# A decoder layer on Trainium2: the output stage joined to the RWKV and end program

## The reference

```python
h = rmsnorm(x, g_pre)
s5_x, s5_z, rw_p, rw_z, pl_x, pl_z, gate_cols = split(h @ w_in)
u_s5 = (s5_mix(s5_x) * silu(s5_z)) @ w_up_s5
u_rw = (rwkv_mix(rw_p) * silu(rw_z)) @ w_up_rwkv
u_pl = (pool_mix(pl_x) * silu(pl_z)) @ w_up_pool
merged = gates[0] * u_s5 + gates[1] * u_rw + gates[2] * u_pl      # gates = sigmoid(gate_cols)
out = merged @ w_o
return x + rmsnorm(out, g_post), new states
```

## Time and profile before

| | us |
|---|---|
| median of three runs | 1428.34 |
| lowest, highest | 1427.19, 1429.24 |
| the profiled execution | 1427.25 |
| its span, first to last instruction | 1425.5 |
| PE busy | 1334.1 (94%) |
| DVE busy | 730.2 (51%) |
| ACT busy | 449.1 (32%) |
| POOL busy | 415.8 (29%) |

### The profile page before, as it was taken

How to read it: one execution, slowest core, us unless ns; L and a number is a source line. 1 busy time by engine, 2 the same in 40 slices (tenths; PEclk the granted TensorE clock), 3 DMA queues, 4 the chain that set the end, 5 groups by cost and what they waited for, 6 DMA issues and landing times. The chain is left out here.

```text
span 1425.5 us, 32230 instructions
## 1 busy us (share of the span) xinstructions
PE 1334.1 (94%) x14048; PEld 1216.8 (85%) x14048; DVE 730.2 (51%) x1489; ACT 449.1 (32%) x809; POOL 415.8 (29%) x414
## 2 busy tenths in 40 slices
PE   5999999997999999999999999999999799796997
PEld 5898989997988989889898889899995699795875
DVE  6495534523445646372736546372635459764042
ACT  7122222121424325252524324252525321111131
POOL 7227556452131312122130313122110132244400
PEclk9999999998999999999999999999988999997999
DMA  8342323233512213131222213121232675433342
GB/s 226 83 108 70 108 70 93 75 97 96 154 59 76 75 43 94 58 94 58 70 67 77 70 54 95 46 82 57 69 147 82 183 230 152 115 89 95 104 153 69
DMA packets 165661, 136.98 MB, mean 96 GB/s; under 512 B 33743, under 2 KB 154624, under 8 KB 165392
## 3 DMA queue, kind: packets, MB, share of 16 engines
q1 hardware_dynamic: 159817, 125.03, 29.7%
q10 hardware_dynamic: 5703, 9.89, 2.2%
HBM read 91.36 MB, written 42.34 MB: 94 GB/s over the span
## 5 line engine op out<-in xcount | busy, mean ns | idle before, releaser
L363 PE MATMUL f_ps<-h_hi,fw_hi 128*128 128x384 f32 (+1 forms) x968 | 341.6, 353 | 20.9 <-ACTq L1333 6.5
L365 PE MATMUL f_ps<-h_hi,fw_lo 128*128 128x384 f32 (+1 forms) x968 | 318.5, 329 | 0.0
L1273 POOL TENSOR_TENSOR fw_lo<-fw,fw_hi 128x1024 fp32r<-128x1024 f32 x46 | 110.4, 2400 | 659.4 <-ACT fw_hi L1331 659.4
L364 PE MATMUL f_ps<-h_lo,fw_hi 128*128 128x384 f32 (+1 forms) x864 | 282.9, 327 | 0.0
L363 PEld LDWEIGHTS f_ps<-h_hi,fw_hi 128*128 128x128 f32 x968 | 183.7, 190 | 37.5 <-issue 16.2
L365 PEld LDWEIGHTS f_ps<-h_hi,fw_lo 128*128 128x128 f32 x968 | 183.9, 190 | 0.0
L364 PEld LDWEIGHTS f_ps<-h_lo,fw_hi 128*128 128x128 f32 x864 | 163.4, 189 | 3.9 <-issue 3.8
L1345 ACT ACTIVATE f_out<-f_ps 128x384 f32<-128x384 f32 (+1 forms) x108 | 51.1, 473 | 248.6 <-PE f_ps L365 248.3
L1702 DVE TENSOR_TENSOR t_m<-t_m,q 128x256 f32<-128x256 f32 (+1 forms) x66 | 27.6, 418 | 174.0 <-PE q L2099 174.0
L363 PE MATMUL proj_ps<-h_hi,fw_hi 128*128 128x384 f32 (+1 forms) x336 | 114.0, 339 | 1.1 <-PEq L229 1.1
L364 PE MATMUL proj_ps<-h_lo,fw_hi 128*128 128x384 f32 (+1 forms) x336 | 110.5, 329 | 0.0
(11 more groups left out here) (436 smaller groups left out, 2876.1 us busy)
## 6 DMA issues: line engine op xcount, KB each, us to landing
fw<-in_w_in_dram SPq DMA_DIRECT2D x50, 512.0 KB, 4.4
projected<-f_out SPq DMA_DIRECT2D x72, 192.0 KB, 2.0
projected<-proj_out SPq DMA_DIRECT2D x17, 544.5 KB, 2.9
f_out<-projected SPq DMA_DIRECT2D x48, 192.0 KB, 2.4
raw<-projected SPq DMA_DIRECT2D x8, 838.5 KB, 6.6
projected<-f_out SPq DMA_DIRECT2D x36, 160.0 KB, 1.8
branch_z<-projected ACTq DMA_DIRECT2D x8, 544.0 KB, 4.8
xt<-in_x_prompt_dram SPq DMA_DIRECT2D x8, 512.0 KB, 5.6
```

Of the source, the lines that this page charges most:

```text
L363: pe.matmul(out, whi, xhi, start=first, stop=False)
L364: pe.matmul(out, whi, xlo, start=False, stop=False)
L365: return pe.matmul(out, wlo, xhi, start=False, stop=last)
L1273: pool.tensor_tensor(wlo[:, g % 2], wst[:, g % 2], whi[:, g % 2].bitcast(F32), ALU.subtract).then_inc(fw_lo, 1)
```

## The change

`phase_out` goes. Its work moves into the engines' orders of `phase_rwkv`:

- **Weights.** `w_o` is loaded by ACT's queue from b = 16 on, into the room of the last two merged blocks (`wo_raw`). ACT makes the high parts (`wo_high`), one per group of units, the last two at b = 22; DVE makes the low parts (`wo_low`) behind the units of the same group, where POOL did it before. The merged blocks 6 and 7 wait for all of it.
- **PE.** Behind the last up unit `out_first` makes tiles 0 and 1: the blocks 0 to 6 of both, then block 7 of both. Then the tiles 2 to 8 follow one by one, half by half. The tiles use four pairs of banks in turn.
- **ACT, DVE.** The norms follow as before, but ACT squares a half as soon as it is done.
- **SP.** Four `x` tiles are loaded ahead instead of two, behind the last up unit, into the room of `early`; the sums go into four tiles of it.
- **Semaphores and rooms.** `phase_start` and `phase_norm` move into the cleanup of the project program and allocate semaphores without releasing them; `gu` gets another room. The cleanup of `phase_rwkv` now stands behind the last store.

The core of the diff:

```diff
 ACT, in the loop over b of phase_rwkv (OUT_AT = 2 * KT = 16):
                     if b > 2 * KT:
+                        if b == 3 * KT - 1:
+                            act.wait_ge(wo_made, KT)
                         merged_high(b - 2 * KT - 1)
+                    if b == OUT_AT:
+                        act.wait_ge(gated, 3 * OUT_AT)
+                        act.wait_ge(p_lo, WB)
+                        act.wait_ge(stored, 16 * 5)
+                        load_wo(0)
+                        load_wo(1)
+                        act.dma_start(gpost[:, :], io["norm_post"].to_broadcast((P, D))).then_inc(gp_loaded, 16)
+                        wo_high(0)
+                    if OUT_AT < b < 3 * KT - 2:
+                        wo_high(b - OUT_AT)
+                        load_wo(b - OUT_AT + 1)
+                    if b == 3 * KT - 2:
+                        load_wo(KT - 1)
+                        wo_high(KT - 2)
+                        wo_high(KT - 1)
                 merged_high(KT - 1)
+                for t in range(TILES + 1):
+                    out_norm(t)
 with:
+                def load_wo(k):
+                    if k >= 2:
+                        act.wait_ge(wo_made, k - 1)
+                    act.dma_start(wo_raw[:, k % 2], io["w_o"][0, k * P:(k + 1) * P, :]).then_inc(wo_loaded[k % 2], 16)
+
+                def wo_high(k):
+                    act.wait_ge(wo_loaded[k % 2], 16 * (k // 2 + 1))
+                    act.activation(wo_hi[:, k], wo_raw[:, k % 2], ACT.Copy).then_inc(wo_split, 1)
+
+                def out_norm(t):
+                    at, n = out_tiles[t]
+                    for h in range(2):
+                        act.wait_ge(o_mm, 2 * t + h + 1)
...
 DVE, behind the units of each group:
+                def wo_low(k):
+                    dve.wait_ge(wo_split, k + 1)
+                    tt(wo_lo[:, k], wo_raw[:, k % 2], wo_hi[:, k].bitcast(F32), ALU.subtract).then_inc(wo_made, 1)
...
+                    if OUT_AT <= b < 3 * KT - 1:
+                        wo_low(b - OUT_AT)
+                    if b == 3 * KT - 2:
+                        wo_low(KT - 1)
 PE, behind the loop:
+                def out_first():
+                    pe.wait_ge(p_out, 3 * WB)
+                    for t in range(2):
+                        for k in range(KT - 1):
+                            if t == 0:
+                                pe.wait_ge(wo_made, k + 1)
+                                pe.wait_ge(m_lo, k + 1)
+                            for h in range(2):
+                                out_mm(t, h, k)
+                    pe.wait_ge(wo_made, KT)
+                    pe.wait_ge(m_lo, KT)
+                    for t in range(2):
+                        for h in range(2):
+                            out_mm(t, h, KT - 1)
+
+                def out_tile(t):
+                    if t == 2:
+                        pe.wait_ge(gated, N_UP)
+                    if t >= 4:
+                        pe.wait_ge(o_normed, 2 * (t - 3))
+                    for h in range(2):
+                        for k in range(KT):
+                            out_mm(t, h, k)
 SP, behind the last gate load:
+                sp.wait_ge(f_mm, UP0 + N_UP)
+                for t in range(XY):
+                    load_x(t)
...
 build:
                 with nc.cleanup_on_exit():
+                    with ExitStack() as nctx:
...
+                        phase_start(nc, io, e)
+                        phase_norm(nc, io, e)
                     phase_project(nc, io, e)
...
             with nc.cleanup_on_exit():
                 phase_rwkv(nc, io, e)
             fctx.close()
-            with nc.sbuf_tensor("merged_hi_kept", [P, KT, NT], F32R, side="right"):
-                phase_out(nc, io, e)
```

More of the change, by code:

```diff
@@ L1027 @@
 POOL_AT = (8, 10, 13, 15)
+XY = 4
+OUT_AT = 2 * KT
 PROD = [((1, 2), 0), ((3, 5), 0), ((3, 5), 1), ((4, 0), 0)]
@@ L1124, in phase_rwkv @@
              "m_hi", "m_lo", "t_loaded", "flip_old", "flip", "tails", "taken", "stored", "p_ready", "p_chain", "p_mm", "p_out", "p_hi", "p_lo")]
+        (wo_split, wo_made, gp_loaded, o_mm, o_sq, o_s1_done, o_root_done, o_rs, o_normed, o_summed) = [sem("o_" + n) for n in (
+            "w_hi", "w_lo", "g_loaded", "mm", "sq", "s1_done", "root_done", "rs", "normed", "summed")]
+        wo_loaded = [sem(f"o_w_loaded{i}") for i in range(2)]
+        xr_loaded, yo_stored = [sem(f"o_x_loaded{i}") for i in range(XY)], [sem(f"o_y_stored{i}") for i in range(XY)]
+        out_tiles = [(t * P, P if t < TILES else NB * NS) for t in range(TILES + 1)]
         yz_loaded = [sem(f"e_yz_loaded{i}") for i in range(2)]
@@ L1955, in _ @@
                         pool_scale(3)
+                    if OUT_AT <= b < 3 * KT - 1:
+                        wo_low(b - OUT_AT)
+                    if b == 3 * KT - 2:
+                        wo_low(KT - 1)
+                dve.wait_ge(gp_loaded, 16)
+                dve.wait_ge(f_mm, UP0 + N_UP)
+                for t in range(TILES + 1):
+                    out_rows(t)
             @block.tensor
@@ L2339, in _ @@
                         pool_products((5, 7, 9, 12).index(b))
[L2342 to L2421, removed]
-                        act.activation(junk[0:n, :], ps[2 * (t % 4) + h][0:n, :], ACT.Square, accum_out=ss[0:n, h, t:t + 1]).then_inc(sq, 1)
-                    act.wait_ge(s1_done, t + 1)
-                    act.activation(root[0:n, t:t + 1], s1[0:n, t:t + 1], ACT.Sqrt, scale=1.0 / D, bias=e.eps[0:n, 0:1]).then_inc(root_done, 1)
-            @block.vector
-            def _(dve):
-                dve.wait_ge(g_loaded, 16)
-                for t, (at, n) in enumerate(tiles):
-                    dve.wait_ge(sq, 2 * t + 2)
-                    dve.tensor_tensor(s1[0:n, t:t + 1], ss[0:n, 0, t:t + 1], ss[0:n, 1, t:t + 1], ALU.add).then_inc(s1_done, 1)
-                    dve.wait_ge(root_done, t + 1)
-                    dve.reciprocal(rstd[0:n, t:t + 1], root[0:n, t:t + 1]).then_inc(rs, 1)
-                    dve.wait_ge(rs, t + 1)
-                    if t >= 2:
-                        dve.wait_ge(y_stored[t % 2], 16 * (t // 2))
-                    for h in range(2):
-                        d = slice(512 * h, 512 * h + 512)
-                        dve.scalar_tensor_tensor(out=yt[0:n, t % 2, d], in0=ps[2 * (t % 4) + h][0:n, :], scalar=rstd[0:n, t:t + 1],
-                                                 in1=gpost[0:n, d], op0=ALU.mult, op1=ALU.mult).then_inc(normed, 1)
-                    dve.wait_ge(x_loaded[t % 2], 16 * (t // 2 + 1))
-                    dve.wait_ge(normed, 2 * t + 2)
-                    dve.tensor_tensor(yt[0:n, t % 2], yt[0:n, t % 2], xt[0:n, t % 2], ALU.add).then_inc(summed, 1)
@@ L2446, in build @@
+                out_first()
+                for t in range(2, TILES + 1):
+                    out_tile(t)
 def build(nc, io, outs):
```

70 lines of the change are left out of this document (61 added, 9 removed).

## The result

| | median us | lowest, highest | profiled execution | its span |
|---|---|---|---|---|
| before | 1428.05 | 1427.19, 1429.24 | 1427.25 | 1425.5 |
| after | 1413.87 | 1412.67, 1415.40 | 1413.0 | 1411.3 |

The ratio is 0.9908 (95% interval 0.9892 to 0.9924), 14.2 us less by the medians. Both executions of the trace, before and after, are near their medians, so they can be compared stage by stage. Two executions of the study lie far off, the profiled one of x1 at 1632 us with a mean clock of 0.746 and one of before at 3746 us, and are left out of every ratio.

A forecast was written before the change was run, and what follows sets the result against it. PE, busy 94% of the span, was taken as the bound. Gains of 14.1 + 2.5 + 0.7 + 0.7 less 1.0 and 4.7 gave 12.3 us less, forecast 1415.5 us, range 1409.8 to 1420.7.

The forecast's parts named there:

- The pause: PE's idle time between the last up unit and the first output matmul goes: 14.1 us gained.
- Slow clock: The first twelve output matmuls no longer run at the low clock left by the pause: 2.5 us gained.
- stall at 1360: PE's wait for the first tile's norm, before the joint group of four tiles, goes: 0.7 us gained.
- The tail: Behind the last matmul, one of ACT's two squares of the last tile leaves the path: 0.7 us gained.
- The cleanup: Clearing semaphores, with barriers, moves from between the stages to behind the last store: 1.0 us lost, bounds 0 and 1.6.
- DVE's subtracts: Eight w_o subtracts on DVE in the late up units make PE late by 4.7 us, bounds 0 and 9.3.
- the walk: Step along DVE's order: product of unit 67 late by 9.8 us, PE late by 4.7 us at unit 71.
- the cover of the four banks: Lag of DVE at unit 67's product that PE's four banks absorb before unit 71 is delayed: 5.1 us.
- DVE does not hold PE: Rival for the late up units: DVE's new work causes no delay of PE; 1410 to 1411 us, chance 0.15.
- DVE holds longer: Rival for the late up units: DVE holds PE for 7 to 10 us; 1418 to 1421 us, chance 0.15.
- Late loads: Rival: w_o loads come late; slower than before from 8.6 us per load, 1430 us at 9.0; chance 0.04.
- The join does not take place: Rival: PE still stands between up units and tile 0 for w_o or merged rows; 1426 to 1428 us, chance 0.03.

The follow-up runs named there:

- x1: Kernel after with the eight low parts of w_o made by POOL instead of DVE, first run; 1415.66 us, ratio 0.9915.
- x3: Kernel after with one wait added: PE begins the output tiles only when the last merged block is split; 1428.78 us, ratio 1.0015.
- x7: Kernel after without the clearing of semaphores and its barriers behind the last store; 1414.68 us, ratio 0.9915.
- x5: Kernel after itself, unchanged, measured a second time; 1414.74 us, ratio 0.9917.
- x2: Kernel after without DVE's eight w_o subtracts, waits and count kept, so the low part is missing from the output; 1410.89 us, ratio 0.9894.
- x6: Kernel after with w_o splits early and spread: DVE's subtracts behind units 48, 49, 51, 52, 62, 65 and twice 68; 1410.24 us, ratio 0.9883.
- x8: Kernel after with the pool branch's last block split before the up weights at b = 15, on ACT and POOL; 1407.93 us, ratio 0.9859.
- x9: Kernel after with the spread splits of x6, the order of x8 and no cleanup; 1405.36 us, ratio 0.9850.
- x11: As x9, but subtracts behind units 50, 51, 53, 61, 63, 65 and twice 68, copies and loads later to match; 1404.66 us, ratio 0.9843.
- x10: Kernel after with the low parts of w_o made by POOL, run once more for its trace; 1415.57 us, ratio 0.9932.
- x4: Kernel after with w_o splits earlier: DVE's subtracts behind units 48, 49, 51, 52, 56, 59, 65 and 68; 1414.79 us, ratio 0.9916.

## Why the prediction was right

The forecast was 1415.5; the medians are 1413.87 and 1414.74, and the profiled execution took 1413.0 where the sum gave 1415.0. By its steps:

1. **The pause (14.1)** is gone to the last tenth: 0.15 us between the last up matmul and the first of tile 0. x3, with one wait put in front of that order, has 10.93 us of it back.
2. **Slow clock (2.5) and 3. stall at 1360 (0.7)**: together 3.2, measured 103.94 - 100.60 = 3.34. x3 gives 2.6 of it back with the pause, so that part is the clock's.
4. **The tail (0.7)**: 0.71.
5. **The cleanup (-1.0, bounds 0 to 1.6)**: 1.4 to 1.5 by x7. My choice was too low: I took 0.6 us off the bound of 1.6 for a block's entry, and nearly the whole bound came.
6. **DVE's subtracts (-4.7)**: the walk was that PE is late by 4.7 us at unit 71. From unit 48 to unit 71 it is 47.59 us before and 1299.48 - 1247.18 = 52.30 after: 4.7. The product of unit 67 was to be 9.8 us late; it is 1298.87 - 1291.43 = 7.4 us later on the clock, 9.8 counted from unit 48. Of the pieces, the wait at b = 17 is 2.04 (2.0), a subtract 1.23 and a gap (1.27), and POOL blocked seven adds up to unit 67 for 12.8 us where I had eight for 13.6. The eight was a miscount: up to the product of unit 67 the trace of before has seven such meetings too. That 4.7 is met this closely is partly luck. The stalls make 3.7 us, and the other 1.0 is the longer low clock in units 48 and 49 (7.03 us against 6.01), which the walk didn't have. The same 1.0 stands in the 9.8: DVE's own lag is 8.8 us, less the cover of 5.1 that is 3.7. So the mechanism of the walk, a lag less the cover of the four banks, is what the traces show, and its size was 1.0 us too high.

The sum of steps 1 to 6 is 12.3, the balance without its first line 11.8. The 2.35 us that the first comparison had on top, and for which the forecast was high by 1.6 us (0.8 against the second measurement), can't be put down to the change: in x5 the same kernel reaches unit 48 at 1252.34, later than before.

Of what was to show it: DVE was to be over 95% busy (97%) and the longest stall under 2 us (1.0), as forecast. The first output matmul, the last and the last store were to come near 1303, 1404 and 1408.8; they came at 1301.34, 1401.94 and 1406.54, early by 1.7 to 2.3 us, most of it the 2.35 us ahead of unit 48. The clock stayed at 1.00 through the stalls (1266 to 1300), as the walk had it. The expected wait of ACT for each `w_o` load, 3.5 to 5 us, is wrong: the loads landed in 3.5 us at the median (4.4 at most), but ACT arrived after most of them; only two waits are in the trace.

**The rivals.** "DVE does not hold PE" fell: the stalls of 3.7 us are in every execution of after, and x2 and x6 show what it would have been, 1410.89 and 1410.24. "DVE holds longer" fell as well. "Late loads" fell with 4.4 us as the longest, half of the 8.6 that it needed. "The join does not take place" is x3, 1428.78 measured against 1426 to 1428.

## What to carry to other kernels

Joining two stages paid here by the pause and by the slow clock behind it, and only because the consumer's order puts the last block that the producer makes last; with a wait in front of that order the weight split moved ahead was worth nothing. Before work is given to an engine in the shadow of another, walk its order in time, as the mean busy share hides where it is full: the same eight subtracts cost PE 3.7 us as one in each group and 0.2 us in the groups that had room. Measure such a term between two marks that leave other effects out: a stretch that began two units earlier mixed in 1.0 us of clock. Gains measured one by one need not add: by the stretch from the copy to the first output matmul, against 59.85 us in x5, x6 gave 4.4 us, x8 7.6 and the two together (x9) 8.1. About 1.0 of the 4.4 is the clock again, which x8 gives back as well. Once a pause is taken away, an engine that had used it to catch up may have no room left; x11 fits this, but no run shows it alone.

## What the runs showed of the hardware

- **The stretch ahead of the change isn't constant.** Between two copies of ACT, at about 1056 and about 1145 us, in code that no kernel here changes, it took 90.2 us in before, 86.7 in the first execution of after, 89.4 in x2 and 90.4 in x5. Unit 48 started between 1247.2 and 1253.9 over the executions with that pause. What makes it vary is open. Single executions can't be compared by their spans to better than some 5 us here; counted from a mark, they agree within 0.4.
- **The low clock outlasts the pause by a varying time.** After the same pause of 6.1 us, unit 49 took 3.05 us in after, 2.72 to 2.97 in x3, x5 and x7, 2.97 in x10, and 2.08 to 2.11 in before, x2, x4 and x6. After and x2 do the same up to the first subtract, behind unit 50, so between these two the kernel does not explain it; what does is open.
- **Where DVE and POOL meet, DVE pays most, but not always alone.** A POOL subtract of 128x1088 took 2.47 us with no DVE work beside it and 2.54 with an add beside it, while that add took 2.43 instead of 0.56. In the steady meetings of x10 it took 2.79 to 2.89. One that began behind a DVE subtract of `w_o` already under way (1265.21, 1.52 us) took 3.54, so there POOL waited. POOL and DVE of after, in order of time:

```profile
1265.60 3.54 POOL L1343 TENSOR_TENSOR h_lo<-early,merged_hi 128x1088 fp32r<-128x1088 f32 x1
...
1283.03 2.54 POOL L1343 TENSOR_TENSOR h_lo<-early,merged_hi 128x1088 fp32r<-128x1088 f32 x1 [2.70 <-ACT merged_hi L1555]
```

```profile
1283.56 2.43 DVE L1959 TENSOR_TENSOR early<-early,up_gu 128x384 f32<-128x384 f32 x1
```
